# Attention at dilations 1 and 16: two of a block's three score groups issued in one batch, and the values turned behind the transposes of the second group

## What is computed

```python
DILATED_PATTERNS = ((128, 1), (512, 4), (2048, 16))
def banded_causal_attention(q, k, v, span):
    ...
    s = jnp.einsum('nbqhd,nbkhd->nbhqk', qb, kb).astype(jnp.float32) * (hd ** -0.5)
    ...
    valid = (dist >= 0) & (dist <= span) & (blk * SWA_BLOCK + kj - SWA_BLOCK >= 0)
    s = jnp.where(valid[None, :, None], s, -jnp.inf)
    m = jnp.max(s, axis=-1, keepdims=True)
    p = jnp.exp(s - m)
    denom = jnp.sum(p, axis=-1, keepdims=True)
    o = jnp.einsum('nbhqk,nbkhd->nbqhd', p / denom, vb.astype(jnp.float32))
```

## Time and profile before

| | |
|---|---|
| median of 3 runs | 2429.5 us (2422.57 to 2429.86) |
| the profiled execution, its own time | 2430.72 us |
| its span in the trace | 2428.9 us |
| TensorE matmul busy | 2356.4 us, 97% of the span |
| weight load busy | 1911.2 us, 79% |
| VectorE busy | 1734.6 us, 71% |
| ScalarE busy | 1127.0 us, 46% |
| GpSimd busy | 951.7 us, 39% |

### The profile page before, as it was taken

How to read it: one execution, slowest core, us unless ns; L and a number is a source line. 1 busy time by engine, 2 the same in 40 slices (tenths; PEclk the granted TensorE clock), 3 DMA queues, 4 the chain that set the end, 5 groups by cost and what they waited for, 6 DMA issues and landing times.

```text
span 2428.9 us, 33264 instructions
## 1 busy us (share of the span) xinstructions
PE 2356.4 (97%) x11802; PEld 1911.2 (79%) x11802; DVE 1734.6 (71%) x2527; ACT 1127.0 (46%) x2006; POOL 951.7 (39%) x752
## 2 busy tenths in 40 slices
PE   7999999999999997999999999999999999999997
PEld 6777888777678776877788888788788888887886
DVE  7454558996365775355888888878988888886655
ACT  6534264332347664224444444544654544445443
POOL 1111013441075871323556565330446565651211
PEclk9999999999999998999999999999999999999999
DMA  4332325553696336366222223398532332237764
GB/s 173 114 107 97 110 86 171 167 169 114 242 329 209 110 102 214 99 226 226 104 109 109 104 109 124 137 303 271 177 138 104 119 115 109 109 109 263 225 192 147
DMA packets 191942, 379.14 MB, mean 156 GB/s; under 512 B 17185, under 2 KB 63009, under 8 KB 182561
## 3 DMA queue, kind: packets, MB, share of 16 engines
q1 hardware_dynamic: 191776, 377.01, 45.6%
HBM read 252.97 MB, written 123.98 MB: 155 GB/s over the span
## 4 chain that ended last, share of the span: by engine, by line
PE 53%; DVE 5%; issue 1%; ACT 1%; DMA 1%; SPq 0%; DVEq 0%; ACTq 0%
PE ff_bank L78 16%; PE ff_bank L80 16%; PE ff_bank L79 16%; PE op_bank L70 2%; PE op_bank L72 2%; PE op_bank L71 2%; DVE ff_ring L2960 1%; DVE ff_b_lo L2902 1%; DMA op_mix_in<-mix_t 0%; SPq L2005 0%; DVE ff_x_first L2981 0%; DVE ff_y_gate L2947 0%; DVE ff_ring L2908 0%; DVE op_x_second L2155 0%; DVE ff_y_val L2947 0%
## 5 line engine op out<-in xcount | busy, mean ns | idle before, releaser
L79 PE MATMUL ff_bank<-ff_b_lo,ff_ring 128*128 128x512 f32 x1232 | 480.3, 390 | 0.0
L78 PE MATMUL ff_bank<-ff_b_hi,ff_ring 128*128 128x512 f32 x1056 | 413.9, 392 | 9.9 <-ACT ff_e L2706 5.3
L80 PE MATMUL ff_bank<-ff_b_hi,ff_ring 128*128 128x512 f32 x1056 | 412.1, 390 | 0.0
L70 PE MATMUL ip_bank<-ip_x_hi,ip_w_hi 128*128 128x512 f32 x736 | 302.8, 411 | 13.2 <-DVE ip_x_lo L719 13.2
L71 PE MATMUL ip_bank<-ip_x_lo,ip_w_hi 128*128 128x512 f32 x736 | 288.9, 393 | 0.0
L72 PE MATMUL ip_bank<-ip_x_hi,ip_w_lo 128*128 128x512 f32 x736 | 288.7, 392 | 0.0
L79 PEld LDWEIGHTS ff_bank<-ff_b_lo,ff_ring 128*128 128x128 f32 x1232 | 232.2, 188 | 48.4 <-issue 0.5
L78 PE MATMUL ff_bank<-ff_ring,ff_ring 128*128 128x512 f32 x616 | 241.4, 392 | 3.0 <-DVE ff_ring L2960 2.9
L78 PEld LDWEIGHTS ff_bank<-ff_b_hi,ff_ring 128*128 128x128 f32 x1056 | 199.0, 188 | 54.9 <-issue 7.5
L80 PE MATMUL ff_bank<-ff_ring,ff_ring 128*128 128x512 f32 x616 | 239.7, 389 | 0.0
L79 PE MATMUL ff_bank<-ff_ring,ff_ring 128*128 128x512 f32 x616 | 239.7, 389 | 0.0
(11 more groups left out here) (316 smaller groups left out, 4943.9 us busy)
## 6 DMA issues: line engine op xcount, KB each, us to landing
ff_raw<-in_slabs SPq DMA_DIRECT2D x44, 1024.0 KB, 4.8
proj_t<-ip_staged SPq DMA_DIRECT2D x92, 256.0 KB, 2.7
a_t<-ff_y_val SPq DMA_DIRECT2D x44, 512.0 KB, 2.6
t_t<-ff_t_sum SPq DMA_DIRECT2D x88, 256.0 KB, 2.0
ff_raw_ring<-t_t SPq DMA_DIRECT2D x56, 256.0 KB, 4.0
ff_raw_ring<-s_t SPq DMA_DIRECT2D x52, 256.0 KB, 3.3
rp_tables<-in_rope SPq DMA_DIRECT2D x24, 512.0 KB, 4.4
ff_raw_ring<-in_w_down SPq DMA_DIRECT2D x46, 256.0 KB, 3.5
```

Of the source, the lines that this page charges most:

```text
L70: pe.matmul(out, w_hi[k], x_hi[k], start=(k == 0), stop=False)
L78: pe.matmul(out, w_hi, x_hi, start=first, stop=False, skip_group_check=resumed)
L79: pe.matmul(out, w_hi, x_lo, start=False, stop=False, skip_group_check=resumed)
L80: return pe.matmul(out, w_lo, x_hi, start=False, stop=last, skip_group_check=resumed)
```

## The change

In turns 0 to 23 the function `scores` is called with a tuple of groups. The groups 0 and 1 are issued together: first all four mask products, then the score products of group 0 and those of group 1. Since both need a free pair of banks, the wait ahead of the batch is that of its last group. The transposes T(j-1,0) and T(j-1,1) follow next to each other, V(j) stands behind them, and W(j-1,1) stands directly ahead of W(j-1,2). The order is now S(j,0 and 1), T(j-1,0), T(j-1,1), V(j), W(j-1,0), T(j-1,2), S(j,2), W(j-1,1), W(j-1,2). Turns 24 on keep their order. The programs of the other engines stay as they were.

```diff
-            def scores(j, g):
+            def scores(j, gs):
...
-                if GROUPS * j + g >= GROUPS * FIRST_1 + 2:
-                    pe.wait_ge(max_ready, GROUPS * j + g - 1)
-                elif GROUPS * j + g >= 2:
-                    pe.wait_ge(probs_ready, GROUPS * j + g - 1)
...
+                n = GROUPS * j + gs[-1]
+                if n >= GROUPS * FIRST_1 + 2:
+                    pe.wait_ge(max_ready, n - 1)
+                elif n >= 2:
+                    pe.wait_ge(probs_ready, n - 1)
...
                 if j < FIRST_1:
-                    for hh in range(2):
-                        pe.matmul(to[:, hh, :], idb[:, :], at, start=True, stop=False)
+                    for g in gs:
+                        for hh in range(2):
+                            pe.matmul(scores_at(j, g)[:, hh, 0:2 * SPAN], idb[:, :], at, start=True, stop=False)
...
+                if now and j < FIRST_1:
+                    scores(j, (0, 1))
+                    if last:
+                        turn_probs(j - 1, 0)
+                        turn_probs(j - 1, 1)
+                    if j < TILES_0:
+                        turn_values(j)
+                    if last:
+                        sums(j - 1, 0)
+                        turn_probs(j - 1, 2)
+                    scores(j, (2,))
+                    if last:
+                        sums(j - 1, 1)
+                        sums(j - 1, 2)
+                    continue
```

More of the change, by code:

```diff
@@ L1730, in turn_values @@
                 ins.then_inc(vt_done, 1)
-            def scores(j, g):
+            def scores(j, gs):
                 pat, r, b = blocks[j]
-                if g == 0:
+                if gs[0] == 0:
                     if pat == 0:
@@ L1743, in scores @@
                             pe.wait_ge(q_staged, j - TILES_0 + 1)
-                if GROUPS * j + g >= GROUPS * FIRST_1 + 2:
-                    pe.wait_ge(max_ready, GROUPS * j + g - 1)
-                elif GROUPS * j + g >= 2:
-                    pe.wait_ge(probs_ready, GROUPS * j + g - 1)
-                at = mask[:, 2 if double(j) else 1 if b else 0, :]
-                to = scores_at(j, g)
+                n = GROUPS * j + gs[-1]
[3 more added lines that the diff above has]
+                    pe.wait_ge(probs_ready, n - 1)
@@ L1750, in scores @@
+                at = mask[:, 2 if double(j) else 1 if b else 0, 0:2 * SPAN]
                 if j < FIRST_1:
-                    for hh in range(2):
-                        pe.matmul(to[:, hh, :], idb[:, :], at, start=True, stop=False)
+                    for g in gs:
+                        for hh in range(2):
+                            pe.matmul(scores_at(j, g)[:, hh, 0:2 * SPAN], idb[:, :], at, start=True, stop=False)
                 n = 2 * SPAN // parts(j)
[L1754 to L1763, removed]
@@ L1764, in scores @@
-                ins.then_inc(scores_ready, 1)
+                for g in gs:
+                    to = scores_at(j, g)
+                    for c in range(parts(j)):
+                        for hh in range(2):
+                            heads = slice(HD * hh, HD * (hh + 1))
+                            if pat == 0:
+                                q = (qk_first if b < 4 else qkv)[heads, 0, g, b * SPAN:(b + 1) * SPAN]
+                                k = (qk_first if b < 4 else qkv)[heads, 1, g, max(b - 1, 0) * SPAN:max(b + 1, 2) * SPAN]
+                            else:
+                                q = q_s[heads, j % 2, g, c * SPAN:(c + 1) * SPAN]
+                                k = k_s[heads, j % 2, g, n * c:n * (c + 1)]
+                            ins = pe.matmul(to[:, hh, n * c:n * (c + 1)], q, k, start=j >= FIRST_1, stop=c == parts(j) - 1)
+                    ins.then_inc(scores_ready, 1)
@@ L1813, in _ @@
                 now, last = j < TURNS, 0 <= j - 1 < TURNS
+                if now and j < FIRST_1:
[13 more added lines that the diff above has]
+                    continue
                 if now:
-                    scores(j, 0)
+                    scores(j, (0,))
                 if last:
@@ L1818, in _ @@
                 if now:
-                    scores(j, 1)
+                    scores(j, (1,))
                 if last:
@@ L1824, in _ @@
                 if now:
-                    scores(j, 2)
+                    scores(j, (2,))
                 if last:
                     sums(j - 1, 1)
-                if j < TILES_0:
-                    turn_values(j)
                 if FIRST_1 <= j - 3 < TURNS:
```

## The result

The changed kernel takes 2432.77 us (median of 18 runs, 2429.58 to 2437.72) against 2428.0 us before (18 runs, 2422.57 to 2433.63). The ratio is 1.0017, with a 95% interval of 1.0009 to 1.0025: 4 us slower, less than the 0.3% that the prediction called a clear change. Its profiled execution, the longest of the 18 with 2437.72 us, has a span of 2435.8 us, 6.9 more than before. One of the twelve executions of a kernel further down ("reordered dilation 1, V(0) late") took 4740.73 us, which nothing here explains, and is left out of that kernel's ratio.

What follows compares the result with a forecast made beforehand. TensorE was taken to set the pace; 0 (dilation 1) + 3.9 (dilation 16) + 3.5 (start) - 2.0 (given back) = +5.4 us, from a median of 2429.5 to 2435 us, range 2426 to 2442.

Steps and rivals of the forecast that it cites:

- TensorE's own saving: On TensorE alone, fewer borders between products and adjacent transposes would save 0.35 us a turn, 8.4 us over 24 turns.
- Dilation 1 stays where it was: In dilation 1 the saving turns into waits of W(j-1,0) and the batch: 0 to -0.03 us a turn, nothing for 15 turns.
- The batch waits for the exponentials of S(j,2): Next turn's batch needs ScalarE's exponentials of S(j,2): it starts at about 7.2 us in dilation 1, 7.5 in dilation 16.
- The sign named for it: In the changed trace, dilation 16 turns of about 7.5 us with the mask products waiting for ScalarE's exponentials.
- Dilation 16, +3.9 us: Dilation 16 turns take 7.5 us against 6.98 at 7 borders, 7.2 at the last; bounds +1.8 and +6.5.
- The start, +3.5 us: In turns 0 and 1, V(0) holds S(0,2) and the batch of turn 1 comes 3.5 us late; taken between +2 and +5.
- the rival of the late clock: At the start the clock rises late: start +6, rest as forecast, +8 us in all, 2437.5 us; chance 0.1.
- Given back, -2 us: Turn 4's 3.0 us wait for a store goes and other VectorE waits shrink: -2 us out of 2.4 and its reloads.
- the batch gives no shorter scores: Rival: T(j-1,0) starts only at 1.86 us and all three answers move by 0.26; +12 us, 2441.5; chance 0.15.
- the gaps are saved and nothing is late: Rival: the full border saving shows in the turns with no late answers; -8.4 us, 2421; chance 0.05.
- the first of its two reasons: Reason against that rival: VectorE's copy of T(j-1,0) can't begin before T has run, with less than 0.1 us to spare.
- weaker form: Rival: dilation 1 gains 0.15 us a turn, dilation 16 loses 2, the start costs 2; about -1, 2428; chance 0.25.

Runs made afterwards that it cites:

- reordered dilation 1, V(0) late: Against the kernel before: batch with T(j-1,0) and its VectorE copy moved first in turns 0 to 15 only, V(0) behind S(0,2); ratio 0.9987.
- reordered version: The changed kernel with T(j-1,0) ahead of the batch and VectorE's copy of it ahead of the maxima of S(j,0); ratio 0.9978 against before.
- T first: The changed kernel with T(j-1,0) ahead of the batch on TensorE alone, VectorE's order kept; ratio 0.9993 against before.
- short exponentials: The changed kernel with the exponentials of S(j,2) in dilation 16 made in two pieces instead of four; ratio 0.9998 against before.
- dilation 1 only: The changed kernel with the old order in turns 16 to 23 (dilation 16); ratio 1.0000 against before.
- batch-only kernel: The changed kernel with V(j) back between W(j-1,1) and W(j-1,2), in turn 0 behind S(0,2); ratio 1.0018 against before.

## Why the prediction was right

It gave 2435 us from 2429.5, +5.4 us, and the measurement is +4.8 us between the medians, +4 us by the ratio, and +5.51 in the attention of the profiled executions. The mechanism is the forecast one in dilation 1 and dilation 16; that the start came out so close is in part luck. Part by part:

- **TensorE's own saving, 0.35 us a turn.** T starts 1.59 us behind the batch; 1.60 was worked out. The saving is reached only where nothing waits: 7.22 to 6.92 us in the reordered version, 0.30 of it. The missing 0.05 is the pair of sums: the prediction left it at 0.94 + 0.84 = 1.78 us, and side by side they take 1.84.
- **Dilation 1 stays where it was (0).** It takes 7.20 us a turn, where 7.17 to 7.2 was given. The cause is the forecast one, W(j-1,0) at 3.03 us where 3.06 was given; this 0.03 and the 0.06 of the pair of sums nearly cancel. That V is its cover is shown by the batch without V's move (7.48 us).
- **The batch waits for the exponentials of S(j,2).** In dilation 16 shown, by shortening them (-0.29 us for 0.30). The sign named for it, a wait of the mask products for ScalarE, is not printed in the trace; the time from the sums to the batch gives it away. In dilation 1 the two paths were said to end together, and the prediction spoke of a wait of the batch there too. The batch starts 0.16 us behind the exponentials' end, where one that is held starts 0.14 behind it, but there is no such wait: the pair of sums takes the same 1.84 us where nothing of S(j,2) is waited for. T first, where W(j-1,0) still waits, leaves the turn at 7.23.
- **Dilation 16, +3.9 us.** +4.14, and returned in full by leaving these eight turns alone.
- **The start, +3.5 us.** +3.31 and +0.29. The delay of the batch was worked out rightly (the batch of turn 1 at 9.28 us, where 638.65 - 629.21 = 9.44 was given). The length of turn 1 was not: I had half of the delay given back because turn 1 does less of its work at the low clock (+2 in all), or more lost if the clock rises late (+5), and took the value between, which no row supported. The clock did rise some 4 us later, so the rival of the late clock had the right fact and too high a price (+6 for the start): +3.6 here, and +3.1 in the run of short exponentials, with the same order and the same 13.7 us at the low clock. Where the clock rose as early as before (dilation 1 only, 10.2 us), the same order costs +2.3. So hitting 3.5 was luck to about 1 us. The idle time ahead of V(0) was 3.35 us and not some 2.5.
- **Given back, -2 us.** Turns 2 to 15 take 2.23 us less, of which 14 x 0.02 = 0.28 is the turn itself and the rest the waits: beyond 14 turns of 7.22 or 7.20 us there were 2.70 us before and 0.75 after. VectorE's wait for the store, 3.0 us before, is gone, as was said.
- The rival *the batch gives no shorter scores* is excluded by T's start. The rival *the gaps are saved and nothing is late* is excluded by the waits, and the first of its two reasons turned out to be a matter of order alone: with T and its copy ahead, dilation 1 does save its gaps. The sum of its weaker form ("about -1") does not follow from its terms: 15 x -0.15, +2 for dilation 16 and +2 for the start make +1.8 us, or -0.2 with the -2 given back.

## What to carry to other kernels

Batching work on the engine that sets the pace makes what stands behind the batch late, and the answers of the other engines with it; add up the chain from the moved instruction through each engine's own queue back to the engine that waits, before counting the saved gaps. If the answer is late, move the question ahead of the batch on the asking engine and the answer ahead in the other's queue: the question alone gained nothing here in dilation 1 (7.23 us), both together 0.28 us a turn; the answer alone was not run. In dilation 16, where the exponentials had held the batch, the question alone gained 0.28. And when turns get shorter, look for the dates that do not move with them (a store that must land, a staging behind loads): here they took back part of each gain. A gain of some us that shows only in one execution's start, where the granted clock differs from run to run, is none until the clocks are compared.

## What the runs showed of the hardware

- Between stretches of 128-row and 64-row products, one pair of borders less saved about 0.3 us a turn of TensorE where nothing else held it (7.22 to 6.92): two groups of scores that stand apart take 2 x 0.95 = 1.90 us, two in a batch 1.59.
- Two groups of sums that stand side by side (8 and 8 passes of 65 columns) took 1.83 to 1.84 us in every run that has them so, and 0.94 and 0.84 with V(j) between them.
- The same order of instructions ran its start with 10.2 or with 13.7 us at 1.2 GHz, from one execution to the next, and three kernels had only 3.4 us there.
- A short wait at the full clock can be followed by a low clock. Behind the wait of 1.25 us ahead of turn 16 (746.37 us) the windows of 2 us show:

```profile
744.00:746.00 2.00, 1.12 (x11) 0.98 (x9) 0.84 (x2) 2.00 (x4) 2.00 (x3) 1.00 0.24 98
746.00:748.00 2.00, 1.63 (x11) 1.20 (x12) 0.40 (x2) 0.57 (x1) 1.85 (x3) 0.69 1.03 422
748.00:750.00 2.00, 2.00 (x12) 1.53 (x14) 1.33 (x2) 0.96 (x4) 0.00 (x0) 0.50 0.29 104
750.00:752.00 2.00, 2.00 (x21) 1.88 (x20) 0.69 (x1) 0.99 (x5) 0.00 (x0) 0.96 0.57 94
```

The clock falls after TensorE is at work again, stays at 1.2 GHz for some 3 us, and rises. The same came behind the wait of 3.27 us in turn 4 of the reordered kernel with V(0) late. The batch-only kernel's wait of 1.63 us in turn 4 was followed by no such fall.
